# Who adds a prompt tile's 128 expert rows: VectorE one of them, TensorE the other 127

## The reference, cut to what matters

```
q = (h @ w_q).reshape(T, PEER_HEADS, 2, PEER_DKH)
s = jnp.einsum('tpsd,psnd->tpsn', q, keys)
...
sc, sel = lax.top_k(cand, PEER_TOPK)
eidx = jnp.take_along_axis(cidx, sel, axis=-1)
gate = jax.nn.softmax(sc, axis=-1)
u = u_tab[eidx]
act = jax.nn.gelu(jnp.einsum('td,tpkd->tpk', h, u))
return jnp.einsum('tpk,tpkd->td', gate * act, v_tab[eidx])
```

## Time and profile before

| | before |
|---|---|
| median of 3 runs | 3315.28 us (3305.32 to 3324.46) |
| profiled execution | 3307.81 us |
| its span in the trace | 3306.1 us |
| mean granted TensorE clock | 0.955 of full speed |
| DVE busy | 2277.6 us |
| gathers | 1152, 1208.03 MB |
| additions by PE | 932 (3728 matmul records) |
| additions by DVE | 220 |

### The profile page before, as it was taken

The page is one execution under the profiler, slowest core; times in us unless marked ns, Lnnn a source line. Parts: engine busy times, 40 slices in busy tenths (PEclk is TensorE's granted clock), DMA queues, the critical chain, the costliest instruction groups (busy, mean ns, idle before and its releaser), DMA issues.

```text
span 3306.1 us, 29878 instructions
## 1 busy us (share of the span) xinstructions
PE 2779.8 (84%) x8950; PEld 1394.0 (42%) x8950; DVE 2277.6 (69%) x5234; ACT 1288.5 (39%) x3786; POOL 1446.7 (44%) x1211
## 2 busy tenths in 40 slices
PE   8988998288978897889788978897899788977877
PEld 5734455144524452445244524452345234522222
DVE  1459779766876787668766876787678766875454
ACT  2135322244345434443453345434533454343333
POOL 5114433345634553446344644564446344643332
PEclk8999999699999999999999999999999999999999
DMA  9489999999999999999999999999999999999998
GB/s 391 162 336 394 379 405 373 383 409 413 421 417 409 414 421 416 402 412 421 416 404 412 421 410 407 419 421 411 416 412 421 417 403 414 421 411 422 422 422 345
DMA packets 190323, 1324.35 MB, mean 401 GB/s; under 512 B 22080, under 2 KB 24768, under 8 KB 37952
## 3 DMA queue, kind: packets, MB, share of 16 engines
q0 software_dynamic: 165888, 1208.03, 88.9%
q1 hardware_dynamic: 16928, 101.86, 7.7%
q10 hardware_dynamic: 7344, 12.55, 1.0%
HBM read 1303.61 MB, written 19.66 MB: 400 GB/s over the span
## 4 chain that ended last, share of the span: by engine, by line
DMA 43%; PE 31%; DVE 11%; ACT 9%; issue 5%; POOL 1%; SPq 0%; ACTq 0%; DVEq 0%
DMA ring_sb<-uv,expert_sb 42%; PE psum L1007 17%; PE psum L758 6%; DVE ring_sb L1487 5%; DVE y_sb L1522 3%; ACT diag_sb L1156 2%; ACT weight_sb L1150 2%; PE psum L980 1%; ACT L1148 1%; ACT weight_sb L1148 1%; ACT front_sb L1076 1%; PE psum L937 1%; DMA ring_sb<-w_q 1%; POOL ring_sb L590 1%; PE psum L917 1%
## 5 line engine op out<-in xcount | busy, mean ns | idle before, releaser
L1007 PE MATMUL psum<-ring_sb,diag_sb 128*128 128x512 f32 x3728 | 1839.2, 626 | 457.5 <-ACT diag_sb L1156 457.0
L590 POOL DMA_INDIRECT ring_sb<-uv,expert_sb x1152 | 1392.2, 1208 | 1793.9 <-PE psum L1007 1308.0
L1487 DVE SCALAR_TENSOR_TENSOR ring_sb<-ring_sb,h_sb 128x1024 f32<-128x1024 f32 x1152 | 1408.7, 1223 | 807.0 <-DMA ring_sb<-uv,expert_sb 795.9
L1007 PEld LDWEIGHTS psum<-ring_sb,diag_sb 128*128 128x128 f32 x3728 | 671.6, 196 | 1421.7 <-ACT diag_sb L1156 843.4
L1148 ACT ACTIVATE weight_sb<-weight_sb 128x1 f32<-128x1 f32 x1152 | 232.6, 202 | 1608.8 <-DVE ring_sb L1487 1600.6
L1156 ACT ACTIVATE diag_sb<-ident_sb,weight_sb 128x128 f32<-128x128 f32 x932 | 374.1, 401 | 76.4 <-PE psum L1007 46.2
L1150 ACT ACTIVATE weight_sb<-weight_sb,gate_sb 128x1 f32<-128x1 f32 x1152 | 339.3, 295 | 37.4
L1522 DVE SCALAR_TENSOR_TENSOR y_sb<-ring_sb,weight_sb,y_sb 128x1024 f32<-128x1024 f32 x211 | 270.3, 1281 | 72.1 <-ACT weight_sb L1150 71.9
L758 PE MATMUL psum<-pool_sb 128*128 128x512 f32 (+1 forms) x672 | 284.8, 579 | 22.4 <-ACT gain_final_sb L1048 22.4
L980 PEld LDWEIGHTS psum<-front_sb,pool_sb 128*128 128x128 f32 x1952 | 248.1, 192 | 87.8 <-issue 85.1
L980 PE MATMUL psum<-front_sb,pool_sb 128*128 128x128 f32 x1952 | 251.3, 275 | 2.2 <-ACT front_sb L1111 2.2
(11 more groups left out here) (186 smaller groups left out, 1584.4 us busy)
## 6 DMA issues: line engine op xcount, KB each, us to landing
pool_sb<-w_in SPq DMA_DIRECT2D x12, 2048.0 KB, 12.0
ring_sb<-uv,expert_sb POOLq DMA_INDIRECT x1152, 12.3
ring_sb<-w_q SPq DMA_DIRECT2D x22, 512.0 KB, 9.7
front_sb<-z SPq DMA_DIRECT2D x8, 1408.0 KB, 10.4
z<-gain_final_sb ACTq DMA_DIRECT2D x40, 256.0 KB, 7.5
pool_sb<-w_q SPq DMA_DIRECT2D x4, 2048.0 KB, 21.7
pool_sb<-w_q SPq DMA_DIRECT2D x10, 512.0 KB, 7.9
x_sb<-x SPq DMA_DIRECT2D x9, 512.0 KB, 8.7
```

Of the source, the lines that this page charges most:

```text
L590: eng.indirect_dma_start(out=uv[SLOT[n]], out_offset=None, in_=dr["uv"], in_offset=bass.IndirectOffsetOnAxis(ap=expert[:, j % 2, k:k + 1], ...
L1007: mm = eng.matmul(bank(b + half), diag[d % DIAGS][:, :], uv[SLOT[n]][:, D + half * BANK:D + (half + 1) * BANK], start=first, stop=last)
L1487: eng.scalar_tensor_tensor(out=u, in0=u, scalar=1.0, in1=h[:, :], op0=ALU.mult, op1=ALU.mult, accum_out=weight[:, k:k + 1]).then_inc(dot_r ...
```

## The change: which rows DVE adds in tiles 1 to 7

```
 def on_dve(n):
     j, k = divmod(n, CHOSEN)
     if j == 0:
         return k > 2 and k < 124
-    if j == TILES - 1:
-        return k == 30
-    return 42 <= k < 48 or (56 <= k < 90 and k % 4 == 2)
+    return k == (30 if j == TILES - 1 else 42)
```

## The result

Changed kernel: 3337.63 us median of 7 runs (3330.76 to 3343.38). Kernel before, on the same chip: 3317.73 us of 7 runs (3305.32 to 3324.46). The ratio is 1.0070, with a 95% interval of 1.0056 to 1.0084, so 19 to 28 us slower, about 23. The profiled execution of the changed kernel took 3343.38 us, with a span of 3341.6.

What follows compares the result with a forecast made beforehand. Gathers on DMA bound this stretch before, PE after the change. PE's 7.95 us of lateness less 3.7 of ring reserve left 4.2 us a tile, 29 in seven tiles; with the 3315 us median, 3344 us, range 3321 to 3368.

Steps and rivals of the forecast that it cites:

- The bound: From the output projection to the end of the queries, PE becomes the bound: 2.69 us a slot against DMA's 2.47.
- PE's path: Tile 4, output projection to row 88's addition: PE ends at 1893.1 against 1885.15, 7.95 us later.
- the change's own repayment: Behind the output projection, rows 48 to 51: PE's 3.68 us wait and 3.0 us of slow clock go, 6.7 us.
- The reserve: At gather 95 of tile 4, the ring hides some 3.7 us of PE's lateness: 11.48 less 7.75.
- the row of gather 36: Tile 4, queue nearly emptied: 7.75 us from issue to use, taken as what a gather needs when PE holds the ring.
- the row of gather 28: Quickest gather found, 5.76 us from issue to use: reserve 5.7 us, loss 2.2 a tile, 16 in all.
- The price of a gather by the Trainium skill: Estimate of 4.4 us for 1.05 MB: reserve 7.1 us, loss 0.9 us a tile, 6 in all.
- The total: Whole kernel: 29 us of loss over seven tiles, 3344 us against the median; chance 0.60 for 16 to 45 us.
- Hidden by the ring: Rival: the ring hides PE's lateness, loss 0 to 2.2 us a tile, 3315 to 3331 us; chance 0.24.
- The loss whole: Rival: gathers late as soon as their queue shortens, 6.5 to 9 us a tile, 3361 to 3378 us; chance 0.11.
- Faster since DVE was the pace: Rival: slots with DVE additions set later landings; removing them gives back 51 us in all, 3264 us; chance 0.05.
- The signs: New profile: DMA share under 1 in the query projection's last third, POOL waiting for PE, tiles 1 to 7 about 4 us longer.

Runs made afterwards that it cites:

- the relieved query projection: Changed kernel, but the query projection of tiles 2 to 8 sums over only the first 512 of its 1024 inputs: 3318.94 us, ratio 1.0018.
- the two pairs: Kernel before and changed kernel, both profiled twice, unchanged; second executions 3310.34 and 3334.08 us. Rows 42 to 96 cost 29.0 us more in the first, 25.4 in the second.
- the six-slot pair: Kernel before and changed kernel, each with six ring slots in place of seven: 3367.17 us (ratio 1.0164) and 3402.73 us (ratio 1.0274).

## Why the prediction was right

**The bound, right.** Behind the output projection PE takes over from DMA: the chain, the 125.89 of 127.30 us, and the relieved query projection all say so.

**PE's path, right almost to the tenth.** Row 88's addition was to end 126.8 us after the projection's start. In tile 4 of the changed kernel gather 95, which that addition frees, is issued 127.30 us after it (1910.56 less 1783.26); in the kernel before 0.51 us lay between the two, and 126.8 and 0.51 make 127.3. The steps hold one by one: additions in the projection, rows 48 to 51 in 7.03 us (forecast 6.88), no wait of 3.68 us, 1.42 us of waiting at row 52 (1.51). The granted clock of 1.00 at rows 48 to 51 was the change's own repayment, as told.

**The reserve, right at the end of the stretch.** Gather 95 and its product in the changed kernel, on POOL and on DVE:

```profile
1910.56 0.94 POOL L588 DMA_INDIRECT ring_sb<-uv,expert_sb  x1 [1.67 <-PE psum L1005]
```

```profile
1918.71 1.21 DVE L1485 SCALAR_TENSOR_TENSOR ring_sb<-ring_sb,h_sb 128x1024 f32<-128x1024 f32 x1
```

From issue to use it is 8.15 us, where 7.75 was forecast and 11.48 stood before. The gather landed 7.5 us after its issue (11.5 before); the rest is DVE, which was still busy with the router. At the first step of the loss, behind the projection, gather 54 took 6.73 us (issued at 1805.49, used at 1812.22). So the reserve was not one number, but the loss of the whole stretch is set at its end, and there the row of gather 36 was the right one to take. It was a choice between two single gathers: the row of gather 28 would have made the sum 16. That the figure fits so closely is in part luck.

From the means of the two pairs PE was 7.5 us late a tile and the loss in rows 42 to 96 is 27.2 us, 3.9 a tile, so 3.6 were hidden (3.8 in the first pair, 3.4 in the second), where the forecast took 3.7 of 7.95. The sum said 29. The price of a gather by the Trainium skill ("DMA: Bandwidth & Descriptors", section "Anatomy of one DMA — SWDGE (gpsimd) path": 2.0 us fixed plus the bytes, about 4.4 us as an estimate) would have made the sum 6. The 6.73 and 8.15 us of the trace do not agree with that price; neither gather was alone in its queue, and no run here shows one that is.

**The total.** Rows 42 to 96 cost 27.2 us, rows 0 to 41 cost 1.9 (768.6 and 770.4, means of two), and rows 97 to 127 took 3.0 less (572.9 and 569.8), where two profiles of the kernel before differ by 2.6. That makes 26.1 for tiles 1 to 7, and the timed runs say 19 to 28. The forecast of 29 above the median was thus some 3 to 6 us too high. No term of the sum is clearly mis-sized: the reserve came out at 3.4 to 3.8 us, and the 2 us between 29 and 27.2 are less than the 2.7 by which two profiles of the kernel before differ in rows 57 to 96. What the sum put at nothing are the rows outside the stretch. The prediction said that the time is not won back behind row 88; some 3 us of it may be, as shown above, and the cause is open. Tile 0 took 452.4 us in both first profiles and tile 8 took 318.4 and 318.6, unchanged as forecast.

**The rivals.** Hidden by the ring: refuted by the 1.0070, though the ring hides about half (3.6 of 7.5 us); that it hides a part, the six-slot pair shows by itself. (The middle of that rival's range, 3315 to 3331, is 3323 and not 3321; nothing hangs on it.) The loss whole, 6.5 us a tile and more: refuted by 3.9. Faster since DVE was the pace: refuted; DVE's products wait for the gathers more than before (909.6 us of idle time on the page, for 795.9), and undoing half of the change brings about half of the time back.

**The signs.** DMA's busy share was to fall under 1 in the last third of the stretch. It does, but only just: 0.98 and 0.99 in two steps of 10 us in tile 4, and 1.00 to 1.01 over the whole stretch, so that the average hides it. The GB/s of the same steps (362 to 393 for some 421) and POOL's wait for PE (1492.0 us on the page, 1308.0 before) say it more plainly.

## What to carry to other kernels

When work moves onto an engine, follow that engine's path through the stretch where the work lands, and ask how late the buffers it frees become and how much lateness the queue behind them can hide: here 13 additions of 1.72 us made PE 7 to 8 us late, the ring hid about half, and the rest was lost in each of seven tiles. An average utilisation is no guide; PE's 84% of the span had no room at this place, while one addition a tile moved from PE to DVE where the transfers ran dry was worth 0.3%. Profile both kernels twice before a difference of a few microseconds in one stretch is given a cause.

## What was unexpected of the hardware

- The busy share of the DMA engines hardly falls when the queue runs short: in the changed kernel 10 us at a share of 1.00 moved 362 GB/s, where before 1.02 went with 424. By these records a byte then occupies the engines for some 15% longer.
- Where PE is the bound its time repeats closely: the seven stretches of the changed kernel from the output projection to gather 95 were 127.30 to 127.31 us long, in both profiles. The same stretches of the kernel before, where DMA is the bound, took 118.51 to 120.62 us.
- The time up to the first product differed by up to 8.8 us between two executions of one kernel (214.7 and 205.9 us for the changed one), which is more than a third of what the change costs.
